# Middle group's cached scores moved from TensorE to GpSimd and VectorE, with a new order in a retention head

## The reference

```python
h = x @ w_in                      # 1024 -> 10240: q, k, v of attention, za, q, k, v of retention, zr, ga, gb
# branch A: 3 groups (window, dilation) = (128,1), (512,4), (2048,16), 4 heads of 128 each
s = q . k(at distances 0, d, .. w) / sqrt(128) - slope * distance;  softmax;  p @ v;  merged over the groups
# branch B: retention, 4 heads, chunks of 128 tokens, per-token causal, with a state of 128 x 256
o = (q k^T * decay) v + q S * decay;   S = decay * S + k^T v;   normalised per head
out = (sigmoid(ga) * (silu(za) * o_a) @ w_pa + sigmoid(gb) * (silu(zr) * o_b) @ w_pb) @ w_o
y = LayerNorm(alpha * x + out)
```

## Time and profile before

| | us |
|---|---|
| median of 3 runs (lowest, highest) | 864.7 (863.86, 865.67) |
| the profiled execution | 867.8 |
| its span, first to last instruction | 866.1 |
| TensorE busy (matmul) | 844.1 (97%) |
| VectorE busy | 446.1 (52%) |
| ScalarE busy | 248.4 (29%) |
| GpSimd busy | 206.7 (24%) |

### The profile page before, as it was taken

The page is one execution under the profiler, slowest core; times in us unless marked ns, Lnnn a source line. Parts: engine busy times, 40 slices in busy tenths (PEclk is TensorE's granted clock), DMA queues, the critical chain, the costliest instruction groups (busy, mean ns, idle before and its releaser), DMA issues.

```text
span 866.1 us, 20033 instructions
## 1 busy us (share of the span) xinstructions
PE 844.1 (97%) x7644; PEld 809.2 (93%) x7644; DVE 446.1 (52%) x799; ACT 248.4 (29%) x370; POOL 206.7 (24%) x181
## 2 busy tenths in 40 slices
PE   7999999999999999999999999999899999999996
PEld 6999999999999999998899797898799999999996
DVE  4437844595438634773545454554463333333467
ACT  4124421441224403342232223312242222222200
POOL 0019301650138002824315105134100000000003
PEclk9999999999999999999999999999989999999998
DMA  6998979876995799677889596796939678877712
GB/s 193 227 273 315 314 206 228 287 270 218 213 354 172 269 203 282 219 259 252 278 311 367 172 388 238 250 370 212 396 118 326 224 268 269 264 268 274 256 49 110
DMA packets 162731, 220.02 MB, mean 254 GB/s; under 512 B 8577, under 2 KB 136321, under 8 KB 160961
## 3 DMA queue, kind: packets, MB, share of 16 engines
q1 hardware_dynamic: 157856, 206.05, 76.0%
q0 software_dynamic: 4176, 11.02, 3.9%
q10 hardware_dynamic: 656, 2.36, 0.7%
HBM read 206.68 MB, written 100.01 MB: 354 GB/s over the span
## 4 chain that ended last, share of the span: by engine, by line
PE 91%; DVE 3%; DMA 2%; issue 1%; ACT 1%; POOL 1%; SPq 0%; POOLq 0%; DVEq 0%; ACTq 0%
PE bank L775 23%; PE bank L777 22%; PE bank L776 22%; PE bank L770 6%; PE bank L805 5%; PE bank L1082 3%; PE bank L900 2%; PE bank L875 2%; PE bank L1134 1%; PE bank L1159 1%; PE bank L1035 1%; PE bank L1122 1%; DMA xn<-in_x_prompt_dram 1%; PE bank L1149 1%; DVE wl L1497 1%
## 5 line engine op out<-in xcount | busy, mean ns | idle before, releaser
L775 PE MATMUL bank<-xh,wh 128*128 128x288 f32 x640 | 193.2, 302 | 0.7 <-DVE vn L1564 0.6
L777 PE MATMUL bank<-xh,wl 128*128 128x288 f32 x640 | 189.5, 296 | 0.0
L776 PE MATMUL bank<-xl,wh 128*128 128x288 f32 x640 | 189.4, 296 | 0.0
L775 PE MATMUL bank<-wh,xh 128*128 128x256 f32 x640 | 184.1, 288 | 1.1 <-DVE wl L1497 0.8
L776 PE MATMUL bank<-wl,xh 128*128 128x256 f32 x640 | 179.4, 280 | 0.0
L777 PE MATMUL bank<-wh,xl 128*128 128x256 f32 x640 | 179.3, 280 | 0.0
L1497 DVE TENSOR_TENSOR wl<-raw,wh 128x1024 fp32r<-128x1024 f32 (+1 forms) x104 | 129.8, 1286 | 9.9 <-ACT wh L1297 9.1
L775 PEld LDWEIGHTS bank<-wh,xh 128*128 128x128 f32 x640 | 121.3, 190 | 4.5 <-issue 2.6
L775 PEld LDWEIGHTS bank<-xh,wh 128*128 128x128 f32 x640 | 121.4, 190 | 1.8 <-issue 1.2
L1297 ACT ACTIVATE wh<-raw 128x1024 fp32r<-128x1024 f32 (+1 forms) x104 | 101.8, 1018 | 74.1 <-PE bank L805 43.5
L776 PEld LDWEIGHTS bank<-xl,wh 128*128 128x128 f32 x640 | 121.5, 190 | 0.1
(11 more groups left out here) (206 smaller groups left out, 1457.8 us busy)
## 6 DMA issues: line engine op xcount, KB each, us to landing
raw<-in_w_in_dram SPq DMA_DIRECT2D x128, 256.0 KB
out_dram<-in_cache_kv_w_dram SPq DMA_DIRECT2D x16, 2040.0 KB, 10.2
out_dram<-in_cache_kv_w_dram SPq DMA_DIRECT2D x32, 1020.0 KB, 9.6
cslot<-in_cache_kv_w_dram SPq DMA_DIRECT2D x24, 1024.0 KB, 8.7
far<-in_cache_kv_w_dram SPq DMA_DIRECT2D x32, 512.0 KB, 9.8
out_dram<-in_cache_kv_w_dram SPq DMA_DIRECT2D x20, 504.0 KB, 10.8
raw<-in_w_in_dram SPq DMA_DIRECT2D x16, 512.0 KB
keyslot<-in_cache_kv_w_dram SPq DMA_DIRECT2D x8, 1024.0 KB, 8.0
```

Of the source, the lines that this page charges most:

```text
L775: pe.matmul(out, lhs[0](k), rhs[0](k), start=(k == 0), stop=False)
L776: pe.matmul(out, lhs[0](k), rhs[1](k), start=False, stop=False)
L777: last = pe.matmul(out, lhs[1](k), rhs[0](k), start=False, stop=(k == n - 1))
```

## The change

Cached middle keys are no longer transposed or scored on TensorE; `keyslot` holds the near tile alone, and `turn_keys`, `key_copy` and a shorter `cached_scores` replace the five-tile versions. In stage A `far` is two halves. Places 0 to 31 hold the middle group's keys of the head, loaded by `middle_keys` where the first half of the far keys was. Places 32 to 63 hold the far group's, 32 at a time: `far_keys(h, 0)` where the second half was, and `far_keys(h, 1)` after eight sums of the head, ahead of chunk c+6. A middle key serves two queries (q and q + 4), so GpSimd makes two products of each piece, the first into a buffer `prod`, the second in place: 16 products and 16 sums a head, not 8. The queries of the middle group are projected first, and turned after unit 11 by two more transposes. One copy of 1 MB a head moves from stage A to stage C. In a retention head the order on TensorE, ScalarE and VectorE is new; `states_out` and `chain_out` are gone.

The core of the diff:

```diff
+            def middle_keys(h):
+                sp.wait_ge(far_summed, h * FAR_PIECES + FAR_PIECES)
+                settle(sp)
+                src = caches[1].rearrange("b (n m j) c h e -> j (b n) m c (h e)", n=4, j=4)
+                for j in range(4):
+                    sp.dma_start(far[j:P:4, 0:FAR_M, :], src[j, :, :, 0, bass.ds(h * DH, DH)]).then_inc(middle_in, 16)
...
             def far_keys(h, half):
-                if half == 0:
-                    sp.wait_ge(far_summed, h * FAR_PIECES + FAR_PIECES)
+                if half == 1:
+                    sp.wait_ge(far_summed, h * FAR_PIECES + (FAR_PIECES + 8))
                     settle(sp)
                 src = caches[2].rearrange("b (n m q) c h e -> q (b n) m c (h e)", q=16, n=2)
-                for q in range(half * FAR_Q, (half + 1) * FAR_Q):
-                    sp.dma_start(far[q:P:DEC_T, :, :], src[q, :, :, 0, bass.ds(h * DH, DH)])\
-                        .then_inc(far_in, 16)
+                m = slice(half * FAR_M, (half + 1) * FAR_M)
+                for q in range(DEC_T):
+                    sp.dma_start(far[q:P:DEC_T, FAR_M:, :], src[q, :, m, 0, bass.ds(h * DH, DH)])\
+                        .then_inc(far_in[half], 16)
...
-                    elif j < 3:
-                        far_keys(h, j - 1)
+                    elif j == 1:
+                        middle_keys(h)
+                    elif j == 2:
+                        far_keys(h, 0)
...
                 columns(h * A_CH + 5, (h * RV + OFF_ZR,), CW)
                 rows(2, 2, h * 510, 510)
                 if first:
                     rows(2, 0, 0, 510)
+                far_keys(h, 1)
                 if last:
                     columns(C0_B, (OFF_QR, OFF_KR), RK)
                 else:
                     columns(h * A_CH + 6, (h * DH + (DH + OFF_K), h * DH + (DH + OFF_K + 512)), DH)
-                for b in range(D_COPY_B, A_COPY_B - 1):
-                    rows(2, b, h * 510, 510)
...
                 store_kv(h, 0)
-                pool.wait_ge(far_row, h + 1)
-                for m in range(0, 64, FAR_PIECE):
-                    if m == 0:
-                        pool.wait_ge(far_in, h * 128 + 128)
-                    a = far[:, m:m + FAR_PIECE, :]
-                    tt(a, a, qrow[:, :].rearrange("p (a e) -> p a e", a=1).to_broadcast([P, FAR_PIECE, DH]),
-                       ALU.mult).then_inc(far_prod, 1)
+                def product(out, of, n):
+                    tt(out, far[:, of:of + FAR_PIECE, :], qrow[:, n:n + 1, :].to_broadcast([P, FAR_PIECE, DH]), ALU.mult)\
+                        .then_inc(far_prod, 1)
+                def middle(k):
+                    m = k * FAR_PIECE
+                    if k:
+                        pool.wait_ge(far_summed, h * FAR_PIECES + (FAR_PIECES + (0, 1, 3, 9)[k]))
+                    product(prod[:, :, :], m, 0)
+                    product(far[:, m:m + FAR_PIECE, :], m, 1)
+                def distant(side):
+                    pool.wait_ge(far_in[side], h * 128 + 128)
+                    for m in range(FAR_M, 2 * FAR_M, FAR_PIECE):
+                        product(far[:, m:m + FAR_PIECE, :], m, 2)
+                pool.wait_ge(far_row, h * 2 + 1)
+                pool.wait_ge(middle_in, h * 64 + 64)
+                middle(0)
+                middle(1)
+                pool.wait_ge(far_row, h * 2 + 2)
+                distant(0)
+                middle(2)
+                middle(3)
+                distant(1)
...
+                    if u == 11:
+                        pe.wait_ge(unit_free, h * A_UNITS + (3 + 11))
+                        pe.wait_ge(o_read, h * QBLK + 1)
+                        for e in range(2):
+                            last = turn(bank[2][:, (2 + e) * P:(3 + e) * P], qdup[:, e, :])
+                        last.then_inc(far_turned, 1)
...
+            def turn_keys(r, x):
+                pe.wait_ge(key_in, r * 32 + (16 * x + 16))
+                settle(pe)
                 for h in range(H):
-                    last = turn(bank[KEY_BANK[j]][:, h * P:(h + 1) * P], keyslot[:, j, h * DH:(h + 1) * DH])
+                    last = turn(bank[2][:, h * P:(h + 1) * P], keyslot[:, h * DH:(h + 1) * DH])
...
-                    def score_tile(j):
-                        pe.wait_ge(key_copied, r * (2 * KTILES) + (KTILES * x + j + 1))
-                        g, variant = (0, 0) if j == 0 else (1, G + j - 1)
-                        for h in range(H):
-                            o = variant * TURNED + h * DEC_T
-                            last = pe.matmul(bank[4][quad(h), g * P:(g + 1) * P], qm[:, o:o + DEC_T],
-                                             keyt[j % KEYT][:, h * P:(h + 1) * P], start=(j < 2), stop=(j in (0, KTILES - 1)))
-                        last.then_inc(key_used, 1)
...
-                        transpose_tile(r, x, j)
+                    pe.wait_ge(key_copied, r * 2 + (x + 1))
                     pe.wait_ge(qm_done, r * 2 + (x + 1))
                     settle(pe)
-                    score_tile(0)
-                    score_tile(1)
-                    transpose_tile(r, x, 4)
-                    for j in range(2, KTILES):
-                        score_tile(j)
+                    for h in range(H):
+                        last = pe.matmul(bank[4][quad(h), 0:P], qm[:, h * DEC_T:(h + 1) * DEC_T],
+                                         keyt[:, h * P:(h + 1) * P], start=True, stop=True)
+                    last.then_inc(key_used, 1)
...
                 cached_probs(0)
+                value_unit(3)
...
                 blocks(lambda t, c: turn(b[:, c], rot[:, t, 0:RK]))
-                value_unit(3)
+                value_unit(4)
                 sample_att()
                 b = group(3)
                 blocks(lambda t, c: turn(b[:, c], rot[:, t, RK:2 * RK]))
                 sample_output()
                 sample_state_pair(0)
-                value_unit(4)
+                turn_keys(r, 1)
+                cached_output(0)
                 sample_state_pair(2)
-                cached_output(0)
+                cached_turn(0)
+                next_unit(0)
                 att_group()
-                cached_turn(0)
-                transpose_tile(r, 1, 0)
-                transpose_tile(r, 1, 1)
                 state_group(0)
                 state_group(1)
                 cached_scores(1)
                 output_group(0)
                 output_group(1)
-                next_unit(0)
+                next_unit(1)
                 cached_probs(1)
-                next_unit(1)
                 next_unit(2)
                 cached_output(1)
                 next_unit(3)
...
+                act.wait_ge(far_summed, h * FAR_PIECES + FAR_PIECES)
+                act.wait_ge(far_turned, h * 2 + 1)
+                act.activation(qrow[:, 0:2, :], bank[2][:, 2 * P:].rearrange("p (n e) -> p n e", e=DH), ACT.Copy)\
+                    .then_inc(far_row, 1)
                 group(2, kt[:, 2, :].rearrange("p (a j) -> p j a", a=2), bank[6][:, :].rearrange("p (j a) -> p j a", a=2))
                 next_high(3)
-                act.wait_ge(far_summed, h * FAR_PIECES + FAR_PIECES)
-                act.wait_ge(far_turned, h + 1)
-                act.activation(qrow[:, :], bank[2][:, P:2 * P], ACT.Copy).then_inc(far_row, 1)
+                act.wait_ge(far_turned, h * 2 + 2)
+                act.activation(qrow[:, 2, :], bank[2][:, P:2 * P], ACT.Copy).then_inc(far_row, 1)
...
-                key_tiles(r, 0, 2, KTILES)
                 rows(0)
                 queries(r, 1)
+                high(C0_C if last else r * B_CH + (C0_B + 2), 0, used_b(5))
                 act.wait_ge(rt_done, r * 18 + 2)
                 act.activation(qrt[:, :], bank[7][:, :], ACT.Copy).then_inc(qrt_done, 1)
                 group(3, krt[:, :], bank[7][:, :])
-                high(C0_C if last else r * B_CH + (C0_B + 2), 0, used_b(5))
+                key_copy(r, 1)
                 cached_output(0)
-                key_tiles(r, 1, 0, KTILES)
...
+                def far_sum(n):
+                    dve.wait_ge(far_prod, h * FAR_PIECES + (n + 1))
+                    if n == 0:
+                        dve.wait_ge(far_free, h + 1)
+                        settle(dve)
+                    near = n // 4 % 2 == 0
+                    x = n // 8 * 4 + n % 4
+                    if near:
+                        k, e = x // 2, x % 2
+                        src = far[:, k * FAR_PIECE:(k + 1) * FAR_PIECE, :] if e else prod[:, :, :]
+                        out = fsum[:, 0, e * FAR_M + k * FAR_PIECE:][:, 0:FAR_PIECE]
+                    else:
+                        m = FAR_M + x % 4 * FAR_PIECE
+                        src = far[:, m:m + FAR_PIECE, :]
+                        out = fsum[:, 1, x * FAR_PIECE:(x + 1) * FAR_PIECE]
+                    dve.tensor_reduce(out, src, AX.X, ALU.add).then_inc(far_summed, 1)
...
                 values(18)
-                far_sum(0)
+                far_sum(6)
```

(7 more changed lines are left out.)

187 lines of the change are left out of this document (87 added, 100 removed).

## The result

The changed kernel takes 889.33 us (median of 4 runs, 888.9 to 894.52) against 865.18 us for the kernel before (863.86 to 866.48): a ratio of 1.0297, 95% interval 1.0277 to 1.0318. It is 24 us slower, where 11 us faster was forecast. The profiled execution took 888.9 us, with a span of 886.8 against 866.1.

The account below looks back on a forecast made before the run. TensorE was taken to bound the kernel nearly everywhere: -29.2 us removed, +4 in retention heads, +14.8 in attention heads, -10.4 in sum, so 867.8 becomes 857.4 profiled, median 854 us; 8-in-10 range 839 to 867.

Parts of the forecast that it names:

- TensorE loses 29.2 us: Removed TensorE work: transposes of `keyslot` 17.5 us, score products 10.7, wait for `keyt` 1.0.
- The gate: Attention heads: far keys queued ahead of chunk c+6's weights delay ScalarE's split and last exponential; 3.7 us a head, 14.8 total.
- point 4: Attention head: ScalarE, in order behind chunk c+6's landing at 191.2, ends the exponential at 196.9; TensorE 3.7 us later.
- my eighth sum: Attention head: VectorE's sum releasing the far-key loads, taken at 175.4, between 173.3 and 176.9; at 176.9, 5.2 us a head.
- the gate would close less (0.27): Rival, chance 0.27: chunk c+6 lands in time for ScalarE in the attention heads; 842 us.
- The pair of wl: Attention head: VectorE's two `wl` ahead of unit 15's copy lose 2.48 us beside GpSimd's products; TensorE waits 0.3 to 0.6.
- the rival had the better price: Rival, chance 0.15: in attention heads each `wl` half waits a whole GpSimd product, 5.2 us a pair; 865 us.
- point 5: Attention head's end: value stores behind the 16th product land at 213, TensorE needs the next copy at 213.3; no cost.
- The rival had the mechanism: Rival, chance 0.09: late far keys delay product 16 and the stores at attention heads' ends, 25 us at three boundaries; 879 us.
- 4 us forecast for `atts`: Retention heads: TensorE waits 0.8 to 1.6 us for `atts` behind two `wl` and a copy; 1.0 taken, four times.
- the other moves keep their cover: Retention heads: softmax chains still have two units, or one unit and two output groups, in front; no cost.
- The moved copy hidden: The copy of 1 MB a head moved from stage A to stage C is hidden by stage C's queue; no cost.

Follow-up runs that it names:

- filling the wait: Changed kernel plus six 128x512 products on TensorE ahead of its wait for the last block's exponential: 891.65 us, ratio 1.0309.
- the kernel of 854 us: Changed kernel with weights ahead of far keys' second turn, value stores ahead of last products, retention low halves and unit copy back, cached and own values ahead of states: 854.08 us.
- the run with ScalarE's order: Changed kernel with ScalarE's last exponential and copy ahead of chunk c+6's split, and VectorE's low part behind the turned probabilities: 885.86 us, ratio 1.0261.

## Why the prediction was wrong

Forecast and measurement of the span are 31 us apart. Stage A has 18.5 of them, 11.2 in waits and 7.3 behind them; stage B has 12.2.

1. **TensorE loses 29.2 us: right.** 21.9 became 5.0, 13.4 became 3.2, and the idle time ahead of the scores fell by 1.0, from 1.8 to 0.8: 28.1. But it was not the wait for `keyt` that went: that fell only from 1.0 to 0.8.

2. **The gate (the 3.7 us of point 4): mechanism right, size wrong, and this is the step that failed.** Place, cause and chain are as forecast, but the exponential ends at 208.2 - 7.5 = 200.7, not at 196.9, and the head comes out of the place 7.5 us later than before, not 3.7. The 3.8 us are three small slips in one direction. The issue of the far keys began at 176.7 in the head's own time, 1.3 later than my eighth sum, though inside the bounds that I had given it (up to 176.9). From that issue to the split took 16.9 us, not 15.8. And ScalarE needed 7.1 us, not 5.7: I had put one half of the chunk behind the landing, but the second landed 0.41 after the first was split, and its 1.06 counts too. I had written down the chance that the gate would close less (0.27), and none that it would close more, beyond the 5.2 us a head of a late sum.

3. **The clock was not in the sum at all.** A wait of 3.5 to 6 us was priced at its length. Behind it TensorE ran at 1.2 GHz, worth 1.45 to 2.63 us a head, as filling the wait showed. Stage A's 33.3 us are then: 25.6 of waits less 0.7 that were there before, 1.1 for eight more turns, and 7.3 left, against the 7.7 that the filling gave back.

4. **The pair of wl: the rival had the better price.** I took 2.48 us for meeting the products, the rival 5.2; it was 4.14 (6.50 against 2.36), and 1.62 to 1.83 us of waiting in place of my 0.3 to 0.6 and the rival's 3. That rival's time of 865 was still wrong, since it rested on the same gate.

5. **The stores (point 5) "just hold": only behind the gate.** In the changed kernel TensorE waits for them nowhere. Without the gate they cost 10.5 us. The rival had the mechanism, its condition (product 16 ends after 202; with the weights first it ended at 208.5, some 205 in the head's own time, whose first scores were wanted at 165.5 in place of 162.1) and too high a price.

6. **The retention heads: 4 us forecast for `atts`, 5.2 found, and it wasn't what cost.** The failed sentence is "the other moves keep their cover". It was argued for the softmax alone. The loads of cached values lost theirs, 4.3 us of 14.5, more than half of it to the move of `next_unit(0)` and the rest to the removed scores and turns. Of stage B's missing 12.2 us (25.2 against 13.0), the values' waits are 6.1, `pm` in the last head 1.5, `atts` 1.2, the smaller removal 1.1. Against them the last head's wait for `rot` fell from 2.3 to 0.5, so 4.1 stay unassigned.

7. **The moved copy hidden: right in the changed kernel (0.3 us of idle time), but not for good.** In the kernel of 854 us, taking it out of that stage made the stage 4.4 us shorter and the median 1.6.

The gain that the forecast counted on is there, 11 us of it, but only with the weights ahead of the far keys, the stores ahead of the products, the low halves back and the values ahead of the states; with the copy back in stage A it is 12. The kernel before was not run with the edits among these that it could take; its TensorE waited at none of these places, but for the 0.59 us of the earlier trace rows.

## What to carry to other kernels

When work leaves an engine or moves on it, list what was issued ahead of that work and used behind it: its cover is what was removed or moved, and no line of the diff names the load. A gate found in a trace hides the next one, so a cure's gain is at most the distance to the next event behind it, and the sum of a chain of small terms needs both ends of each, since slips in one direction add up. A wait of some microseconds on TensorE is to be priced above its length where the trace shows the clock falling behind such waits.

## What the runs showed of the hardware

- The granted clock was at half (seven turns 1.75 us against 0.93) behind waits of 5.46 us and the like, and full behind waits of 1.6; filling the wait kept it full. Between them it went either way: in the run with ScalarE's order the clock of the next 2 to 3 us was 1.00 behind a wait of 2.93 us, 0.73 behind 2.78, 0.52 behind 3.06 and 0.50 behind 3.26. The four waits of 3.55 to 5.98 us cost 7.7 us on top of their length.
- A pair of wl took 2.34 us with GpSimd idle, 4.84 and 4.53 beside a run of products, and 6.50 where one product ran at its start and the next began at 167.01. Of the products beside the 6.50, the one at its start took 2.40 us, the next 2.63 and the one at 169.60 took 3.35; one beside a later pair took 3.37.
- With thirty-six more instructions in a loop the instruction packets rose from 28 to 47, and TensorE was idle 5.77 and 5.68 us at the starts of the third and the fourth head.
